# Modulation blocks in the stops of the layer norms, and a second expert layer with a ring of eight whose outputs add up in PSUM

## The reference, cut to what matters

```
# first stack, for each layer i
m = silu(c) @ w_mod[i] + b_mod[i]                   # 9 blocks of 1024: shift, scale, gate, three times; the same with c_ctx
h = layer_norm(ALPHA*h + 0.5*m[2] * swiglu(h*(1+m[1]) + m[0]), ...)
y = attention(h*(1+m[4]) + m[3])                    # layer 0: neighbourhood, with a bias table; layer 1: window
h = layer_norm(ALPHA*h + m[5]*y, ...)
h = layer_norm(ALPHA*h + 0.5*m[8] * swiglu(h*(1+m[7]) + m[6]), ...)
# second stack, for each layer l
m = silu(c) @ w_ada[l] + b_ada[l]                   # 6 blocks of 1024
x = x + m[2] * mixer(rms_norm(x)*(1+m[1]) + m[0])
g, idx = top_k(softmax(hh @ w_router), 32)          # each of the 16 experts takes 32 tokens
y[e] = (silu(xs[e] @ w_gate[e]) * (xs[e] @ w_up[e])) @ w_down[e] * g[e]
x = x + m[5] * scatter_add(y, idx)
```

## Time and profile before

| what | value |
|---|---|
| median of 3 runs | 2965.43 us (2954.81 to 2967.33) |
| profiled execution | 2961.48 us, span 2959.8 us |
| PE busy | 2690.8 us, 91% |
| DVE, ACT, POOL busy | 43%, 30%, 7% |
| mean granted TensorE clock | 0.952 of full |
| moved by DMA | 527.54 MB, 178 GB/s over the span |

### The profile page before, as it was taken

One profiled execution on the slowest core, in us unless ns is written; L12 is line 12 of the kernel. 1 busy time (PEld: TensorE's weight loads), 2 busy tenths in 40 slices (PEclk: granted clock), 3 DMA queues, 4 the chain that ended last, 5 costly groups with the idle time before them and its releaser, 6 DMA issues. The chain is left out here.

```text
span 2959.8 us, 42379 instructions
## 1 busy us (share of the span) xinstructions
PE 2690.8 (91%) x15366; PEld 1911.8 (65%) x15366; DVE 1279.8 (43%) x2123; ACT 898.0 (30%) x1425; POOL 221.9 (7%) x372
## 2 busy tenths in 40 slices
PE   5999997998899999899999777997988998798887
PEld 4777785665677778677777556996666433466323
DVE  4333355444533335533335656566543232563112
ACT  1222225443422212422222544345433100433100
POOL 0110002221011010010110000000000000000000
PEclk9999998999899999999999888997998999899998
DMA  7764433332275573475664214764104699515997
GB/s 265 239 199 147 127 91 71 70 76 83 79 239 181 162 228 98 129 227 157 191 219 113 49 38 129 224 189 135 50 22 162 290 427 427 169 43 230 428 427 298
DMA packets 428523, 527.54 MB, mean 178 GB/s; under 512 B 29718, under 2 KB 382484, under 8 KB 415988
## 3 DMA queue, kind: packets, MB, share of 16 engines
q1 hardware_dynamic: 392884, 399.69, 39.1%
q0 software_dynamic: 35520, 126.24, 13.4%
HBM read 524.83 MB, written 1.05 MB: 178 GB/s over the span
## 5 line engine op out<-in xcount | busy, mean ns | idle before, releaser
L1847 DVE TENSOR_TENSOR wlo<-raw,whi 128x1024 fp32r<-128x1024 f32 x392 | 478.1, 1224 | 470.9 <-ACT whi L1397 446.3
L1397 ACT ACTIVATE whi<-raw 128x1024 fp32r<-128x1024 f32 x392 | 413.4, 1056 | 579.3 <-PE bank L699 521.4
L697 PE MATMUL bank<-xhi,whi 128*128 128x512 f32 (+1 forms) x1568 | 581.3, 371 | 3.0 <-DVE xlo L2364 3.0
L698 PE MATMUL bank<-xlo,whi 128*128 128x512 f32 (+1 forms) x1568 | 565.3, 361 | 0.0
L699 PE MATMUL bank<-xhi,wlo 128*128 128x512 f32 (+1 forms) x1568 | 562.9, 359 | 0.0
L697 PEld LDWEIGHTS bank<-xhi,whi 128*128 128x128 f32 x1568 | 296.2, 189 | 97.8 <-issue 55.3
L699 PEld LDWEIGHTS bank<-xhi,wlo 128*128 128x128 f32 x1568 | 296.6, 189 | 46.6
L698 PEld LDWEIGHTS bank<-xlo,whi 128*128 128x128 f32 x1568 | 296.7, 189 | 40.8 <-issue 0.7
L1299 PE MATMUL bank<-experts,xsT 128*64 128x512 f32 (+1 forms) x1024 | 238.6, 621 | 35.6 <-DMA experts<-in_w_up 32.6
L697 PE MATMUL bank<-hhi,whi 128*128 128x512 f32 (+1 forms) x704 | 255.9, 363 | 0.2 <-DVE hlo L1954 0.2
L699 PE MATMUL bank<-hhi,wlo 128*128 128x512 f32 (+1 forms) x704 | 255.3, 363 | 0.0
(11 more groups left out here) (304 smaller groups left out, 3297.9 us busy)
## 6 DMA issues: line engine op xcount, KB each, us to landing
raw<-in_ffn_w_in SPq DMA_DIRECT2D x176, 512.0 KB, 4.3
mod_ring<-in_w_mod POOLq DMA_DIRECT2D x128, 512.0 KB, 4.3
experts<-in_w_gate SPq DMA_DIRECT2D x32, 2048.0 KB, 23.4
experts<-in_w_up SPq DMA_DIRECT2D x32, 2048.0 KB, 19.5
experts<-in_w_down SPq DMA_DIRECT2D x32, 2048.0 KB, 21.8
mod_ring<-in_w_ada POOLq DMA_DIRECT2D x96, 512.0 KB, 4.7
raw<-in_ffn_w_out SPq DMA_DIRECT2D x64, 384.0 KB, 3.5
raw<-in_ffn_w_out SPq DMA_DIRECT2D x64, 320.0 KB, 3.1
```

The lines of the kernel that those rows point to most:

```text
L697: pe.matmul(o, wh, hi[:, k0 + k, cols], start=(first and k == 0), stop=False)
L698: pe.matmul(o, wh, lo[:, k0 + k, cols], start=False, stop=False)
L1397: act.activation(whi[:, slot, :], raw[:, slot, :], ACT.Copy).then_inc(*n.mark("hi_ready"))
L1847: dve.tensor_tensor(wlo[:, slot, :], raw[:, slot, :], whi[:, slot, :].bitcast(F32), ALU.subtract)\
```

## The change

Twelve of the 28 blocks leave the loops. `RIDERS` keeps 4, 2, 7 and 3 blocks; `FILLERS` names two blocks for each of the six layer norms, 16 steps. PE runs 4 of them ahead of `h_ready`, 2 behind the mean, 3 behind the sums of squares, 4 behind L798, and the last 3 behind `first_products` (in the last norm 7 behind L798). The two blocks add up in banks 6 and 7 and are turned later by `turn_fillers`: behind the fourth unit in a feed-forward part, behind the first scores in `neighbourhood`, ahead of `window`, and at the end. POOL loads the steps through the same ring of four; before `bt` is touched, `ring_read` waits until all steps were used. At stop 5 the first four steps are issued ahead of POOL's wait for `h_ready` and of the two loads of `ctx_2`, the others behind.

In the second expert layer the ring has eight slots (a new one of 16 KB, slot 7, used first). Pair 0 also spreads the gate over partitions (`spread_gate`, 8 matmuls of 128 columns, copied by ACT to `gate_row`) and puts `h`, tokens on partitions, into banks 4 to 7 (`residual_rows`, 16 matmuls of 128 columns). DVE multiplies both halves of `down`'s result by the gate into `ysb`, and `add_outputs` adds into banks 4 to 7 (4 matmuls of 512 columns a pair). At the end DVE and ACT copy two banks each to `outT`, and four DMAs of 256 KB store it. The first expert layer stays as it was.

```diff
-RIDERS = ((("w_mod", 0, 2, 7),), (("w_mod", 1, 0, 9),), (("w_ada_2", 0, 0, 6), ("w_ada_2", 1, 0, 4)), (("w_ada_2", 1, 4, 2),))
+RIDERS = ((("w_mod", 0, 2, 4),), (("w_mod", 1, 1, 2),), (("w_ada_2", 0, 0, 6), ("w_mod", 1, 7, 1)), (("w_ada_2", 1, 1, 3),))
+FILLERS = ((("w_mod", 0, 6), ("w_mod", 0, 7)), (("w_mod", 0, 8), ("w_mod", 1, 0)), (("w_mod", 1, 3), ("w_mod", 1, 4)),
+           (("w_mod", 1, 5), ("w_mod", 1, 6)), (("w_mod", 1, 8), ("w_ada_2", 1, 0)), (("w_ada_2", 1, 4), ("w_ada_2", 1, 5)))
-RING_SLOTS = (5, 6, 0, 1, 2, 3, 4)
+RING_SLOTS = ((5, 6, 0, 1, 2, 3, 4), (7, 5, 6, 0, 1, 2, 3, 4))
...
+            def fill(steps=2 * KD):
+                for _ in range(steps):
+                    if not fillers:
+                        return
+                    name, j, k = fillers.pop(0)
+                    if k == 0:
+                        acquire(6 + j)
+                    pe.wait_ge(*n.next(f"mod_full{k % MOD_RING}", 16))
+                    mod_step(6 + j, k, mod_ring[:, k % MOD_RING, :], name)
+            def turn_fillers(rows):
+                for b, row in zip((6, 7), rows):
+                    evacuated(b)
+                    pe.sem_inc(s[f"bank_ready{b}"], 1)
+                    acquire(b)
+                    passed()
+                    turn_row(b, row)
...
                             first_products(range(3), cols, before)
+                            fill()
                             acquire(3)
                             product(3, unit(), KD, 0, xhi, xlo, cols, True, True)
+                            if after_norm:
+                                turn_fillers(product_rows)
...
-            def layer_norm(cols):
+            def layer_norm(cols, steps):
+                fillers.extend((name, j, k) for j, (name, _, _) in enumerate(FILLERS[fill_no[0]]) for k in range(KD))
+                fill_no[0] += 1
+                fill(steps[0])
                 pe.wait_ge(*n.next("h_ready"))
...
+                fill(steps[1])
+                inverse_root(cols, steps[2])
+                fill(steps[3])
...
+                def add_outputs(p, rounds):
+                    for r in rounds:
+                        half, t = r // 2, r % 2
+                        if t == 0:
+                            evacuated(2 + half)
+                        mm = pe.matmul(bank[4 + r][:, :], st[0:HD, p, t * P:(t + 1) * P], ysb[0:HD, half * 512:(half + 1) * 512],
+                                       start=False, stop=(p == PAIRS - 1), skip_group_check=True)
...
                     if p == 0:
                         turn_places()
+                        if not ctx_too:
+                            spread_gate()
+                            residual_rows()
                     turn()
                     down(p)
...
+            def ring_read():
+                for q in range(4):
+                    pool.wait_ge(*n.peek(f"mod_used{q}", MOD_RING))
             ride(RIDERS[0])
+            ride_fillers(0)
+            ring_read()
             pool.wait_ge(*n.next("inputs_loaded", N_LOADS * 16))
             pool.wait_ge(*n.next("x_ready", 2 * KD))
...
+            ride_fillers(4, 0, MOD_RING)
             pool.wait_ge(*n.next("h_ready", 5))
             ...
+            ride_fillers(4, MOD_RING)
             ride(RIDERS[3])
+            ride_fillers(5)
+            ring_read()
```

More of the change, by code:

```diff
@@ L738, in input_tiles, with up_down @@
                 return before
-            def up_down(cols, riders, new_cond=False, new_context=False):
+            def up_down(cols, riders, new_cond=False, new_context=False, after_norm=True):
                 before = input_tiles()
-                for kind, half, start, reps, m in ffn_loops(riders):
+                for kind, half, start, reps, rider in ffn_loops(riders):
                     nf = HALVES[half][1]
-                    m = m is not None
+                    m = rider is not None
                     if kind == "down" and start == 0:
@@ L1468, in up_down @@
                                     mod_row()
+                                if f and after_norm and (kind, half, start) == ("up", 0, 0):
+                                    filler_rows(product_rows)
                                 units(1)
@@ L1795, in combined @@
                 def combined(rounds):
-                    for r in rounds:
+                    for r in rounds if ctx_too else ():
                         for g in range(nt // 2):
@@ L1811, in _ @@
                         places_turned()
+                        if not ctx_too:
+                            for half in range(2):
+                                act.wait_ge(*n.next("gate_row"))
+                                act.activation(gate_row[:, half * 512:(half + 1) * 512], bank[2 + half][:, :], ACT.Copy).then_inc(*n.mark(f"bank_read{2 + half}"))
+                            own()
+                            act.sem_inc(s["gate_moved"], 1)
                     act.wait_ge(*n.next("hid_turned"))
@@ L1816, in _ @@
                     passed()
-                    act.activation(ysb[0:nt * CAP, 0:512], bank[2][0:nt * CAP, :], ACT.Copy).then_inc(*n.mark("bank_read2"))
+                    if ctx_too:
+                        act.activation(ysb[0:nt * CAP, 0:512], bank[2][0:nt * CAP, :], ACT.Copy).then_inc(*n.mark("bank_read2"))
+                    else:
+                        n.next("bank_read2")
                     n.next("bank_read3")
+                if not ctx_too:
+                    for half in range(2):
+                        act.wait_ge(*n.filled(5 + 2 * half))
+                        act.activation(outT[:, 1, half * 512:(half + 1) * 512], bank[5 + 2 * half][:, :], ACT.Copy).then_inc(*n.mark("out_copied"))
+                    return
                 combined(range(4))
@@ L1956, in up_down @@
                             mod_columns(7, *rider[0:2], i + rider[2])
+                        if filler is not None and (kind, half, start) == ("up", 0, 0):
+                            fillers(filler)
                         if new_context and (kind, half, start) == ("up", 0, 0):
```

212 lines of the change are left out of this document (136 added, 76 removed).

## The result

The changed kernel takes 2943.38 us at the median of four runs (2935.95 to 2947.14), the kernel before 2961.53 beside it: a ratio of 0.9939 with an interval of 0.9920 to 0.9958. It is faster, by 18 us where about 50 were forecast, and outside the range of 2892 to 2932 us. The profiled run of after is the shortest of its four: 2935.95 us, span 2934.3, which is 25.5 less than the span of before.

A forecast was written before the change was run, and what follows sets the result against it. TensorE, busy for 91% of the span, was taken as the bound outside its gaps. Loops -63, stops +23, second experts -3.7 and the end -8 us made -51.7; forecast 2912 us, range 2892 to 2932.

The forecast's parts named there:

- The loops: Feed-forward loops: 13 blocks fewer at 5.4 us each, one more in FFN 4 at 6.8 us, net -63 us.
- The delay of the bias: Stop 1: POOL's wait `ring_read` makes the bias 9.0 us late; the stop costs 7.5 us in place of 1.8.
- The second experts and the end: Second expert layer -3.7 us, and a shorter end behind the last `down`, -8 us.
- the term for the slot: Second expert layer: an eighth slot gives -4.9 us, less about 1.2 us of DMA idling, net -3.7 us.
- Stop 4: Stop 4, as each of stops 1 to 4, was to cost +1.8 us, bounds -1.5 and +5.
- Step 5 needs the slot of step 1, so its load is issued at about t0+0.8 and lands 4.3 us later: Stops, counted from the last product's end (t0): step 5's load lands at t0+5.1; TensorE waits from t0+3.7.
- the term of stop 5: Stop 5: late loads delay L798 and the steps behind it, +6 us, bounds +2 and +11.
- that of stop 6: Stop 6: all 16 steps run before `h_ready`, which comes 4 us later; bounds 0 and +9.
- The ring starves the stops: All stops, 18 ring turns: slower landings, up to 2998 us; chance of slower 0.03, of half way (2937 us) 0.08.
- the turns, which were forecast: On TensorE's path in each of stops 1 to 4: two turns at about 0.45 us.
- 0.5 less was forecast: Stops 1 to 4: the stop up to the first tile stays as long as it is, -0.5 us.
- a clock that stays up: Six stops: the steps keep TensorE's clock up, gaining 11 us, 2901 us in all; chance 0.15.

The follow-up runs named there:

- stop_1_empty: Changed kernel with stop 1 empty, its two blocks back in the loop of the first feed-forward part: 2946.62 us, ratio 0.9945 to the kernel before.
- ring_of_seven: Changed kernel with the second expert layer's ring back at seven slots: 2951.61 us, ratio 0.9969 to the kernel before.
- no_filler_loads: Changed kernel with the stops' steps reading a constant table, their loads not made: 2903.03 us, ratio 0.9794 to the kernel before.
- half_loads: Changed kernel with each load of the stops' steps moving half the columns, read twice by TensorE: 2916.25 us, ratio 0.9861 to the kernel before.
- sums_first: Changed kernel with one block per stop, steps 5 to 8 behind the sums of squares, columns taken earlier, stop 5's context loads last: 2926.92 us, ratio 0.9878 to before.

## Why the prediction was wrong

**Right.** The loops gave what they should: 15.7 us for three riders (16.2), an iteration with a rider behind another still 27.15 us. The delay of the bias (8.6 us late, 9.0 forecast; the stretch +9.7, 7.5 forecast) was read from the queue of GpSimd and shown by `stop_1_empty`. The second experts and the end were right in sum (-12.5, -11.7 forecast). In the term for the slot the prediction's own numbers (2752.7 and 2753.1) give 0.4 us of idle time and not 1.2, so -4.5; the runs have 3.7 by place and 5.8 by `ring_of_seven`. Stop 4 looks right too (+1.9, +1.8 forecast), but that is partly the luck of this trace: five others with the same code there have some 2 to 5 us.

**The step that failed** is this one: "Step 5 needs the slot of step 1, so its load is issued at about t0+0.8 and lands 4.3 us later". From it the turns of the ring in all six stops were worked out. 4.3 us is the median of loads made while the loops ran. The DMA engines are 73% busy there too (the window of FFN 1 above), but a slow load holds up next to nothing (0.3 us of waits in all). In a stop four loads are issued one behind the other and each is waited for: the medians are 4.9 to 5.6 us, the longest 7.0 to 9.6. The trace of the kernel before showed it where it mattered: the four loads behind the mean of stop 5 took 5.7 to 8.6 us.

In stops 1 to 4 the error is small. The prediction has step 13 done 17 us behind the last product; in stop 1 it is 17.7. In stop 5 it has step 5 begin 6.9 us behind the mean, L798 at 12.4 and step 13 done at 17.4; measured are 8.0, 14.6 and 22.9. In stop 6 it has step 5 5.1 us behind the last product and step 16 done at 19.8; measured are 7.1 and 28.1, some 7 us for a turn of the ring in place of 5. So the term of stop 5, +6, measures some 11, and that of stop 6, +4, measures 12 to 13. The direct proof that the loads cost this is `no_filler_loads` (-40 us, by the ratios -43) and `half_loads` (-27, by the ratios -23) against the changed kernel, with the stops of their traces.

The bytes of the steps alone would not have told it. The experts' stream moves 2 MB in 4.92 us, so 512 KB need 1.23 us, and twelve of them behind a first landing of about 5 us end some 20 us behind the last product: an estimate that agrees with the 19.8 of the prediction and not with the 28.1. What else is to be moved in that stretch, and the turns, come on top.

**The rival half seen.** "The ring starves the stops" names the mechanism, and even the landing, 5.7 us, that stops 5 and 6 show at the median, but it got 0.08 since "in stop 1 only one weight unit is under way, and the ring is otherwise alone". The ring alone fills the DMA engines (2% busy before, 99% now), and the argument was made from stop 1 for all stops: in stop 5 they were full already, and stop 6 begins with weight units of the next stack.

**Not seen:** the first rider's wait for DVE's columns behind stops 2 and 3. With the slower clock behind it and the longer turn ahead of it, it makes the iteration 4.3 and 2.7 us longer, 7.0 of the 11.2 us missing there; 0.9 of these are the turns, which were forecast. The later first tile (1.5 us in stop 2, 2.7 in stop 3, where 0.5 less was forecast) gives the rest. This is a second cause beside the loads: the two stretches are only 0.5 us shorter each without them.

**The clock.** The prediction gave 0.15 to a clock that stays up. Without loads it does in part: stops 1 to 4 last 14.3 us, 1.1 less than the empty ones of before, with a granted clock of 1.00 up to the wait for the first tile, where it falls to 0.76 to 0.82 in windows of stops 2 and 3. That this kernel comes to 2903 us, near the 2901 of that rival, is chance, since it lacks the loads. With the loads the holes of 1 to 7 us are back, and the granted clock falls to 0.50 to 0.53 in windows of stops 3, 5 and 6; the eight records of a step then last 1.08 us in place of 0.64. What the clock alone costs there was not separated from the waits.

## What to carry to other kernels

Work moved into a stall brings its own transfers. Price them by the landing times of loads that were made in that very stall, by the bytes that must pass within it, and by the turns of their ring; a median over a stretch where the landing was hidden says nothing of it. In these runs the first block in a long stop, half of whose steps were loaded when it began, was nearly free, and the second gave no more than it took. Look at the windows of the stall itself too: in stops 1 to 4 the DMA engines were at most 2% busy before the change, in stop 5 and as stop 6 began they were full, and these two paid 13 us each in the traces where the others paid at most 3. And whatever takes the results must come in time: here DVE's place for them held up the next rider.

## What the runs showed of the hardware

A load of 512 KB by GpSimd landed in 3.6 to 9.6 us in the stops, depending on what else was under way, one of 256 KB in 2.9 to 6.4. With four issued in a row in stop 5 of `sums_first` the steps that waited for them came 1.3 us apart, at 410 GB/s. Whether TensorE's clock stays up went with the waits, but not with their length alone: the same nine steps of stop 5 fitted into 9.2 us with a granted clock of 1.00 (2.4 GHz) when they had no loads to wait for; with waits for loads they took 22.9 us and ran in part at 0.50 (1.2 GHz; 1.08 us for a step's eight records, not 0.64). Behind one and the same wait of 2.23 us the clock fell in all of seven traces in FFN 2 and in three of them in FFN 3.
